# Loading the last up-projection piece of a mixture-of-experts layer as 16 transfers of 8 partitions

## What is computed

```
h  = RMSNorm(x)
group, then the 2 best of its 8 experts     # per token; 4 groups x 8 = 32 experts
hid = silu(h @ w_gate[e]) * (h @ w_up[e])   # w_gate, w_up: (32, 2048, 512)
y  += gate * (hid @ w_down[e])              # w_down: (32, 512, 2048)
x  = x + y
```

## Time and profile before

| | us |
|---|---|
| median of 3 runs | 1474.69 |
| lowest, highest | 1468.80, 1481.01 |
| the profiled execution | 1476.93 |
| its span, first to last instruction | 1474.9 |
| TensorE, mean granted clock | 0.902 of full |
| TensorE busy | 1161.9 (79%) |
| VectorE, ScalarE busy | 614.6 (42%), 206.5 (14%) |
| HBM read | 475.67 MB |

### The profile page before, as it was taken

The page is one execution under the profiler, slowest core; times in us unless marked ns, Lnnn a source line. Parts: engine busy times, 40 slices in busy tenths (PEclk is TensorE's granted clock), DMA queues, the critical chain, the costliest instruction groups (busy, mean ns, idle before and its releaser), DMA issues.

```text
span 1474.9 us, 19686 instructions
## 1 busy us (share of the span) xinstructions
PE 1161.9 (79%) x8497; PEld 594.6 (40%) x8497; DVE 614.6 (42%) x1286; ACT 206.5 (14%) x442; POOL 15.8 (1%) x31
## 2 busy tenths in 40 slices
PE   6999999999999988965764877757765677667666
PEld 5885564656785543322221322222222222222222
DVE  4878999677554443321222222311231123212312
ACT  2202012273001421100000100000000000000000
POOL 4000000000000000000000000000000000000000
PEclk9999999989999988988886998887998888878888
DMA  9333452610637578999999999999999999999996
GB/s 310 129 143 114 158 200 107 226 53 29 228 115 265 200 285 348 427 427 427 426 429 427 426 428 426 428 426 429 427 426 427 427 428 426 428 427 427 427 427 260
DMA packets 73525, 479.04 MB, mean 325 GB/s; under 512 B 14886, under 2 KB 21414, under 8 KB 45153
## 3 DMA queue, kind: packets, MB, share of 16 engines
q1 hardware_dynamic: 72176, 477.45, 79.0%
q0 software_dynamic: 864, 0.25, 0.1%
q10 hardware_dynamic: 400, 0.10, 0.0%
HBM read 475.67 MB, written 2.11 MB: 324 GB/s over the span
## 4 chain that ended last, share of the span: by engine, by line
PE 48%; DMA 44%; DVE 4%; ACT 3%; issue 1%; SPq 0%; DVEq 0%; ACTq 0%
DMA ring<-in_moe_w_up_dram 31%; PE bank L648 10%; PE bank L1143 9%; DMA ring<-in_moe_w_down_dram 6%; DMA late_ring<-in_moe_w_up_dram 6%; PE bank L669 5%; PE bank L930 5%; PE bank L1109 3%; PE bank L1190 2%; PE bank L921 2%; PE bank L1039 2%; PE bank L1177 2%; PE bank L1005 1%; PE bank L632 1%; ACT hT L1316 1%
## 5 line engine op out<-in xcount | busy, mean ns | idle before, releaser
L1143 PE MATMUL bank<-ring,x_gathered 128*32 128x256 f32 x2432 | 292.5, 435 | 124.5 <-DMA late_ring<-in_moe_w_up_dram 82.6
L2378 DVE TENSOR_TENSOR tokens_out<-tokens_out,bank 128x512 f32<-128x512 f32 x240 | 148.9, 682 | 440.7 <-PE bank L1190 440.7
L1143 PE MATMUL bank<-late_ring,x_gathered 128*32 128x256 f32 x1664 | 237.7, 436 | 84.7 <-DMA ring<-in_moe_w_up_dram 84.5
L1143 PEld LDWEIGHTS bank<-ring,x_gathered 128*32 128x32 f32 x2432 | 130.3, 123 | 239.1 <-issue 207.5
L1143 PEld LDWEIGHTS bank<-late_ring,x_gathered 128*32 128x32 f32 x1664 | 104.1, 123 | 159.0 <-issue 140.0
L648 PE MATMUL bank<-ring,hT 128*128 128x512 f32 (+2 forms) x416 | 156.1, 536 | 3.1 <-ACT hT L1316 2.6
L1109 PE MATMUL bank<-x_tok,select 128*32 128x512 f32 x512 | 115.9, 1032 | 6.1 <-DVE select L2407 3.2
L648 PEld LDWEIGHTS bank<-ring,hT 128*128 128x128 f32 x416 | 78.6, 190 | 78.0 <-issue 67.0
L2334 DVE TENSOR_TENSOR x_gathered<-bank,gain_cols 128x512 f32<-128x512 f32 x32 | 22.1, 692 | 185.5 <-PE bank L1128 185.5
L669 PE MATMUL bank<-hT,ring 128*128 128x256 f32 x384 | 85.7, 385 | 4.0 <-DMA ring<-in_w_in_dram 2.2
L1190 PE MATMUL bank<-y_slots,weight_slots 32*128 32x512 f32 x496 | 83.1, 745 | 6.7 <-DVE tokens_out L2378 5.2
(11 more groups left out here) (426 smaller groups left out, 1115.4 us busy)
## 6 DMA issues: line engine op xcount, KB each, us to landing
ring<-in_moe_w_gate_dram SPq DMA_DIRECT2D x36, 2048.0 KB, 38.3
ring<-in_moe_w_up_dram SPq DMA_DIRECT2D x35, 2048.0 KB, 43.6
ring<-in_moe_w_down_dram SPq DMA_DIRECT2D x35, 2048.0 KB, 38.5
late_ring<-in_moe_w_up_dram SPq DMA_DIRECT2D x25, 2048.0 KB, 42.6
late_ring<-in_moe_w_gate_dram SPq DMA_DIRECT2D x24, 2048.0 KB, 38.6
late_ring<-in_moe_w_down_dram SPq DMA_DIRECT2D x23, 2048.0 KB, 38.4
ring<-in_w_in_dram SPq DMA_DIRECT2D x20, 1024.0 KB, 9.7
ring<-in_w_out_dram SPq DMA_DIRECT2D x16, 1024.0 KB, 5.7
```

Source lines behind the costliest of these rows:

```text
L1143: mm = pe.matmul(gu_bank[SLOTS * c:SLOTS * c + SLOTS, 0:256], XGT[:, at, k % 4, k // 4, :], pieces[c // 2][:, a:a + 256], start=k == 0, st ...
L2378: ins = v.tensor_tensor(y, x, mix[c][:, :], ALU.add)
```

## The change

Piece 135, until now one transfer of 128 partitions, is issued as 16 transfers of 8 partitions each (128 KB, 8 runs of 16 KB), one after another on the same queue and into the same slot. Each adds 16 to the slot's semaphore, so TensorE waits for 15 x 16 more. Nothing else changes: the bytes, their place, and the order of all other transfers are as before.

```diff
+        ROWS, BY_ROWS = 8, MAIN_PIECES - 3
...
+                elif g == BY_ROWS:
+                    for r in range(0, P, ROWS):
+                        sp.dma_start(shape4(moe_slot(i)[r:r + ROWS, :], q),
+                                     moe_source(j, q)[r:r + ROWS, :, :]).then_inc(main_in[i], 16)
                 else:
                     sp.dma_start(shape4(moe_slot(i), q), moe_source(j, q)).then_inc(main_in[i], 16)
...
-                    return main_in[slot], 16 * uses + (16 if g >= MAIN_PIECES - 2 else 0)
+                    return main_in[slot], 16 * (uses + (P // ROWS - 1 if g == BY_ROWS else g >= MAIN_PIECES - 2))
```

## The result

The changed kernel takes 1492.64 us (median of 4 runs, 1491.35 to 1494.20) against 1473.56 us (median of 4 runs, 1468.80 to 1481.01). The ratio is 1.0128, with a 95% interval of 1.0094 to 1.0161: 19 us slower, outside the range of 1468 to 1481 and on the other side of zero than forecast. The profiled execution has a span of 1490.1 us, 15.2 us longer than before.

A forecast was written before the change was run, and what follows sets the result against it. Weight loading bounds the experts' part, and piece 135's landing sets the end. Landing -0.6 us, SP's queue 0 and an unchanged tail gave 1476.3 us for the profiled execution, 1474.1 as median; range 1468 to 1481.

The forecast's parts named there:

- The tail: TensorE's work from the landing of piece 135 to the end, 23.9 us, said not to change.
- the half rate of the earlier trace: At the very end, 239 then 209 GB/s until about 1460.5, read as engines ending their shares at different times.
- part (1): Where piece 135's bytes go: eight engines get 16 rows, eight none; landing moves -0.6 us, ends -3.2 and +4.9.
- the early ones: Seven engines ending at 1451.2 and a ninth at 1455.0; taking piece 135 they give -0.6 us, chance 0.57.
- one instance: A 12 KB store's eight 1.5 KB rows avoided the engine that carried the q8 packet; on another queue than SP's.
- all eight early: Likeliest case: the 16 transfers use the seven early engines and the ninth; -0.6 us, 1474.1 us, chance 0.57.
- all eight late: Rival: the 16 transfers use the eight engines that q8 uses, without slack; +4.9 us, 1479.6 us, chance 0.11.
- The narrow destination: Rival: eight engines writing 8 neighbouring partitions get two engines' rate, 53 GB/s; +25 us, 1500 us, chance 0.10.
- the rule of the lowest-numbered engines: Trainium skill: a transfer uses the lowest-numbered engines, as many as divide its slowest dimension; always the same eight here.
- SP's queue: Part (2): issuing 16 transfers takes 6.9 us with 8.3 us of cover; cost 0, at most +3 us.
- the late engines' lag: Eight engines end the weights at 1460.5, 9.3 us after the seven at 1451.2; put mostly on q8's instruction packets.
- theory D2: From the experiments: partitions 0 to 63 and 64 to 127 are each fed at the rate of eight engines.

The follow-up runs named there:

- the spread form alone: Only rows 64 to 127 of piece 135 loaded, 8 transfers of 8 rows 4 apart, against the kernel before: 1485.21 us, ratio 1.0086.
- rows spread on both sides: Changed kernel, but each of 16 transfers takes 8 rows 4 partitions apart in source and destination: 1488.52 us, 1.0104 against the kernel before.
- The lower half spread: Only rows 0 to 63 of piece 135 loaded, 8 transfers of 8 rows 4 apart, against the kernel before: 1472.94 us, ratio 0.9998.
- the 64-partition version: Piece 135 in 2 transfers of 64 partitions, against the kernel before: 1486.00 us, ratio 1.0074.
- the 128-partition version: Piece 135 in 16 transfers of all 128 partitions, 1 KB per partition, against the kernel before: 1474.87 us, ratio 1.0012.

## Why the prediction was wrong

**Right: what bounds the end.** The landing of piece 135 sets it. The tail was said to stay 23.9 us and is 1490.1 - 1465.1 = 25.0, from TensorE's lower granted clock after the long wait. Nothing new turned up behind it: TensorE waited for the up piece alone.

**Right: the half rate of the earlier trace rows is engines without work**, and the small transfers appear on SP where they should.

**The step that failed** is in part (1): "Piece 135 then gives eight engines 16 rows of 16 KB in place of 8 (+131 KB each, 131 / 26.7 = 4.9 us)". It prices a row by the engine that carries it, at the engine's steady rate, whatever partition it goes to. The runs showed that this rate holds only where the engines keep apart in the destination. A row to a lower partition, 4 apart from its neighbours in the transfer, moves at the full rate (419 to 434 GB/s over all engines, in four kernels). Transfers of eight rows to neighbouring partitions, or to the upper half, halve the rate of all 16 (200 to 242). The changed kernel does both: its lower half is written in neighbours (alone +9.2 us), its upper half by such transfers too (+11.7 us for the spread form alone). 9.2 + 11.7 = 20.9, against 21.4 measured, but that they add up is in part luck: for rows spread on both sides the same addition gives 0.7 + 11.7 = 12.4 us against 15.1 measured, and each half alone loads 1 MB less than the whole piece.

**The choice of the eight engines was wrong too.** I took them for the early ones from one instance. The lower half spread showed two late ones among them, so that neither of the prediction's cases, all eight early or all eight late, was there. By my sum, a late engine with 8 rows more would have cost +4.9 us, so even with an undisturbed destination -0.6 us wasn't to be had. How much of the 21.4 us comes from this wasn't measured by itself.

**The narrow destination was the right rival and got 0.10.** Its price of +25 us was near to the 21.4, in part by luck, since its picture was another. It had the piece alone run at 53 GB/s and the rest go on; in fact all engines slowed down, to 200 GB/s together, also those on other pieces. I held against it that the engines would fan out as each goes on to its next partitions. They don't in 20 us of half rate, and that argument overlooked the upper half, where rows that are spread are slow as well (+11.7 us).

The Trainium skill, page "SBUF — State Buffer", section "Door 1: The DMA port swizzle", gives four neighbouring partitions (and those 32 further) one port of 16. The runs fit: 8 partitions that are 4 apart in the lower half reach eight different ports there, and are fast; neighbours reach two. Its figure for partitions 0 to 63, 218 GB/s, is close to the 208 and 206 GB/s that all engines moved together while spread rows went to the upper half and under the 250 of the 64-partition version. The Trainium skill, page "DMA: Bandwidth & Descriptors", section "The descriptor swizzle", says that engines 0 to 7 serve partitions 0 to 63 of an ordinary transfer and engines 8 to 15 the others. With the rule of the lowest-numbered engines, which the prediction cites, this would put the eight of a small transfer onto their own ports for the lower half and onto others' for the upper. The fast lower and the slow upper half are as these rules of the Trainium skill have it; no run shows engine numbers or ports.

**SP's queue** was mis-sized: 6.9 us said, 19.4 measured, and longer stalls behind. As said, it cost nothing; the 42.6 us of the 128-partition version show that more cover was there than I had worked out.

**The order of the cases.** The trace had a row on 8 partitions, with 1.5 KB each, and none with large rows. A case with no row and a written rule for it, in a part where both the piece and all that follows it are at the limit of loading, should have been given more than the 0.10, and the range should have reached to it. The sentence that a difference under 1% can't be told from none was wrong too: the intervals here are 0.2 to 0.4% to each side, and 1.28, 0.79 and 0.74% stand clear of none.

No kernel here that loads the whole piece was faster than the one before. These transfers didn't even out the late engines' lag; whether others could, no run shows.

## What to carry to other kernels

In a stream of loads like this one, transfer over all 128 partitions, and if a transfer must be cut, cut it along the free dimension: 16 transfers of 128 x 1 KB cost nothing, 16 of 8 x 16 KB cost 19 us, and even 2 of 64 partitions cost 11 us. A DMA share near 1 with half of the usual GB/s was engines that hold each other up, a share near 0.5 with as many GB/s was missing work; look at both numbers. In a stretch that is bound by loading, the loss was final ten experts before the end too.

## What I had not expected

A collision slows every engine, those on ordinary pieces too: 16 engines at a share of 0.96 moved 200 GB/s together. With the upper rows spread, that is what theory D2 had said beforehand, the rate of eight engines, 8 x 26.7 = 213 GB/s (208 measured), though it doesn't say why no engine at all had a fast packet there. With the lower rows in neighbours D2 doesn't explain it: while that piece's rows went to the lower half, no 16 KB packet on any engine took under 0.97 us, those of ordinary pieces included, where 0.61 is the time at full rate. Where this coupling is, wasn't found, and how much of the loss the two late engines add wasn't measured.

Two transfers of 64 partitions on one queue, with the same bytes on every engine, took the rate of all engines down to 250 GB/s in place of 427.

An upper source into lower partitions, rows out of place by 64, ran at 427 GB/s: which rows of HBM an engine reads made no difference here.
